# A longer ring of weight chunks in the expert stage of a two-block transformer kernel

## The reference, cut to what matters

```python
g_gate, g_idx = lax.top_k(softmax(t @ w_rg + b_rg), 1)            # best of 4 groups
e_w, e_idx = lax.top_k(softmax(e_logits_of_that_group), 2)        # best 2 of its 8 experts
combine = sum(one_hot(expert_id, 32) * weight[..., None], axis=1)
hid = silu(einsum('td,edf->tef', tk, w1)) * einsum('td,edf->tef', tk, w3)   # 1024 -> 256
hid = hid * c[:, :, None]
y = einsum('tef,efd->td', hid, w2)                                # 256 -> 1024
```

## Time and profile before

| | |
|---|---|
| time, median of 3 runs | 1983.52 us (1982.03 to 1984.95) |
| the profiled execution | 1986.33 us, its span 1984.3 us |
| TensorE matmul busy | 1829.4 us, 92% of the span |
| VectorE / ScalarE / GpSimd busy | 900.6 / 590.2 / 719.3 us |
| HBM read / written | 248.11 / 16.78 MB |
| chain that ended last | TensorE 84%, VectorE 7%, DMA 4% |
| granted TensorE clock, mean | 0.960 |

### The profile page before, as it was taken

One profiled execution on the slowest core, in us unless ns is written; L12 is line 12 of the kernel. 1 busy time (PEld: TensorE's weight loads), 2 busy tenths in 40 slices (PEclk: granted clock), 3 DMA queues, 4 the chain that ended last, 5 costly groups with the idle time before them and its releaser, 6 DMA issues.

```text
span 1984.3 us, 22984 instructions
## 1 busy us (share of the span) xinstructions
PE 1829.4 (92%) x8562; PEld 1338.8 (67%) x8562; DVE 900.6 (45%) x1267; ACT 590.2 (30%) x1085; POOL 719.3 (36%) x413
## 2 busy tenths in 40 slices
PE   5999979999997898898789898999988979999999
PEld 3888757776875343433367776777766868888887
DVE  4220666664534132322333465999647664303331
ACT  2322334453332111010123234555435222212221
POOL 4444323333430000000023236788743425444442
PEclk8999989998997899999979898999998989999999
DMA  5222212223332789898632323121243313222221
GB/s 193 96 84 91 81 64 80 80 83 130 117 122 71 286 312 338 313 338 322 250 128 85 127 85 101 64 80 66 69 167 125 128 53 117 96 96 96 96 96 43
DMA packets 82660, 266.33 MB, mean 134 GB/s; under 512 B 9088, under 2 KB 10112, under 8 KB 82560
## 3 DMA queue, kind: packets, MB, share of 16 engines
q1 hardware_dynamic: 61632, 222.33, 32.6%
q10 hardware_dynamic: 18624, 34.21, 4.9%
q0 software_dynamic: 2304, 8.39, 1.3%
HBM read 248.11 MB, written 16.78 MB: 133 GB/s over the span
## 4 chain that ended last, share of the span: by engine, by line
PE 84%; DVE 7%; DMA 4%; issue 2%; ACT 2%; ACTq 1%; SPq 0%; POOL 0%; DVEq 0%
PE psum L519 81%; DMA ring<-stream 4%; DVE root L1728 1%; PE psum L1106 1%; DVE area_r L1702 1%; ACTq L1639 1%; PE psum L816 1%; PE psum L610 1%; DVE area L2232 1%; DVE root L1707 1%; ACT root L1249 0%; ACT area L1249 0%; DMA area<-xT 0%; DVE yt_lo L2041 0%; PE psum L777 0%
## 5 line engine op out<-in xcount | busy, mean ns | idle before, releaser
L519 PE MATMUL psum<-area_r,ring_hi 128*128 128x512 f32 (+1 forms) x3168 | 1001.5, 398 | 18.2 <-DVE area_r L1702 11.7
L420 POOL TENSOR_TENSOR ring_lo<-ring,ring_hi 128x1024 fp32r<-128x1024 f32 x220 | 534.3, 2432 | 1003.0 <-ACT ring_hi L1249 1003.0
L519 PEld LDWEIGHTS psum<-area_r,ring_hi 128*128 128x128 f32 x3168 | 595.1, 191 | 162.9 <-issue 28.0
L519 PE MATMUL psum<-area_r,ring_lo 128*128 128x512 f32 (+1 forms) x1584 | 621.3, 392 | 0.0
L1249 ACT ACTIVATE ring_hi<-ring 128x1024 fp32r<-128x1024 f32 x220 | 231.8, 1057 | 625.2 <-PE psum L519 596.8
L519 PEld LDWEIGHTS psum<-area_r,ring_lo 128*128 128x128 f32 x1584 | 302.0, 191 | 63.3
L519 PE MATMUL psum<-ring,area 128*64 128x512 f32 x768 | 190.5, 620 | 46.1 <-DMA ring<-stream 19.9
L1249 ACT ACTIVATE area<-psum 128x512 f32<-128x512 f32 (+3 forms) x257 | 124.9, 512 | 202.0 <-PE psum L610 71.4
L1728 DVE RECIPROCAL root<-root 128x512 f32<-128x512 f32 (+1 forms) x30 | 94.1, 3137 | 137.9 <-ACT root L1249 137.9
L519 PEld LDWEIGHTS psum<-ring,area 128*64 128x64 f32 x768 | 51.2, 139 | 143.9 <-issue 136.1
L519 PE MATMUL psum<-area 128*64 128x128 f32 (+6 forms) x832 | 112.1, 346 | 15.9 <-DVE area L1729 9.7
(11 more groups left out here) (209 smaller groups left out, 1579.7 us busy)
## 6 DMA issues: line engine op xcount, KB each, us to landing
ring<-stream SPq DMA_DIRECT2D x420, 512.0 KB, 3.8
area<-gates ACTq DMA_DIRECT2D x40, 256.0 KB, 6.2
gates<-root ACTq DMA_DIRECT2D x24, 256.0 KB, 2.0
gates<-area ACTq DMA_DIRECT2D x16, 256.0 KB, 3.6
area<-xT SPq DMA_DIRECT2D x8, 256.0 KB, 8.1
area<-xT ACTq DMA_DIRECT2D x8, 256.0 KB, 3.3
tokens<-area ACTq DMA_DIRECT2D x2, 1024.0 KB, 4.2
x_kept<-area ACTq DMA_DIRECT2D x8, 256.0 KB, 5.6
```

The source lines that it names most:

```text
L420: nc.gpsimd.tensor_tensor(ring_lo[:, c % RS, :], ring[:, c % R, :], ring_hi[:, c % RS, :].bitcast(F32), ALU.subtract).then_inc(w_lo, 1)
L519: return nc.tensor.matmul(out, lhsT, rhs, start=first, stop=last)
```

## The change

The expert stage gets a ring of twelve chunks (`RM = 12`): the six slots of `ring`, one pair of slots over the unused end of `ring_lo`, and two pairs over the tiles of `xt`. Chunks of the first six places are loaded one by one as before; those of the last six are loaded two at a time, by one DMA of 1 MB into a pair of slots, with a semaphore for each pair (`more0` to `more2`). The first of these is issued when chunk 79 has been used, the other two when the turned tokens have been written to HBM (`tok_kept`). The second buffer of fetched rows goes, since `xt` is now taken; each of the four parts of the one buffer is fetched again when the previous group's rows in it have been transposed. The broadcast weights of `dense` move to other tiles. Many semaphores are shared (`z_out` and `g1_out` become `bank_read`, `x1_out` and `x3_out` become `x_added`, `va_out` and `vb_out` become `v_out`, `lam_ok` is counted in `lam_e`, `g1_in` and `g2_in` become `gates_in`, `x_spilled` is counted in `stored`), with their counts shifted.

```diff
+RM = 12
+def landed(c):
+    if c < MOE0:
+        return c // R + 1
+    if c < MOE1:
+        return (MOE0 + (c - MOE0) % RM) // R + (c - MOE0) // RM + 1
+    return c // R + 1 - (MOE1 - MOE0) // R + (MOE1 - MOE0) // RM
...
-        rows_in = [area[:, b:b + 8, :].rearrange("p (q a) b -> p q (a b)", q=PAIRS) for b in (24, 16)]
+        rows_in = area[:, 24:32, :].rearrange("p (q a) b -> p q (a b)", q=PAIRS)
...
+        ring2 = [nc.alloc_sbuf_tensor_at(f"more{x}", [P, 2, CH], F32, offset=at) for x, at in enumerate(
+            (high_at + 4 * 512 * (NT + 2 * PAIRS), area_at + 2048 * XT, area_at + 2048 * (XT + 4)))]
...
-            segment(MOE0 + R, MOE1 + R, weights_used, R - 1)
+            def load_two(c, x):
+                sp.dma_start(ring2[x][:], stream[bass.ds(c, 2)].rearrange("a p n -> p a n")).then_inc(S(f"more{x}"), 16)
+            sp.wait_ge(weights_used, MOE0)
+            load_two(MOE0 + R, 0)
+            sp.wait_ge(S("tok_kept"), 32)
+            for x in (1, 2):
+                load_two(MOE0 + R + 2 * x, x)
+            with sp.Fori(0, (MOE1 - MOE0) // RM - 1) as t:
+                for i in range(R):
+                    sp.wait_ge(weights_used, t * RM + (MOE0 + i + 1))
+                    load(t * RM + (MOE0 + RM + i), (MOE0 + i) % R)
+                for x in range(3):
+                    sp.wait_ge(weights_used, t * RM + (MOE0 + R + 2 * x + 2))
+                    load_two(t * RM + (MOE0 + RM + R + 2 * x), x)
+            for c in range(MOE1, MOE1 + R):
+                sp.wait_ge(weights_used, c - RM + 1)
+                load(c, c % R)
...
-                    if g >= 2:
-                        pool.wait_ge(S("sp_g"), 2 * PAIRS * (g - 1))
+                    if g:
+                        pool.wait_ge(S("sp_g"), 2 * (PAIRS * (g - 1) + q + 1))
...
-                    pe.wait_ge(loads[c % R], 16 * (c // R + 1))
-                    return ring[:, c % R, :]
+                    return arrived(c, 0)
...
+            def arrived(c, turns):
+                i = (c - MOE0) % RM
+                if i < R:
+                    pe.wait_ge(loads[(MOE0 + i) % R], 16 * landed(c) + turns)
+                    return ring[:, (MOE0 + i) % R, :]
+                x, half = divmod(i - R, 2)
+                pe.wait_ge(S(f"more{x}"), 16 * ((c - MOE0) // RM + 1) + turns)
+                return ring2[x][:, half, :]
```

More of the change, by code:

```diff
@@ L186, in block_program @@
         VA = K
-        HF, HG, CBT = 48, 8, 16
+        HF, HG, CBT = 48, 8, 24
         SQ1, XG, XT, LS = 48, 32, 16, 56
@@ L237, in block_program @@
         NB = {"n1": 0, "nx": 1, "nm": 2, "nf": 3}
-        for name in ("va_sq", "va_ss", "va_root", "va_out", "u_out", "z_mm", "z_out", "vb_out", "lam_e", "lam_ok",
-                     "gate_raw", "gate_kept0", "gate_kept1", "g1_in", "g1_act", "g1_out", "x1_out", "lg_mm", "rt_max", "rt_exp", "rt_out", "ctt", "ct_out",
+        for name in ("va_sq", "va_ss", "va_root", "v_out", "u_out", "z_mm", "bank_read", "lam_e",
+                     "gate_raw", "gate_kept0", "gate_kept1", "g1_act", "x_added", "lg_mm", "rt_max", "rt_exp", "rt_out", "ctt", "ct_out",
                      "ct_dram_ok", "cb_in", "fb_silu", "fb_c", "fb_hid", "fb_y", "fb_add", "merged",
                      "pos_mm", "consts2", "flag_ok", "x1_sq", "xg", "xt_t", "xt_out", "tok_kept", "lg_act", "lg_t", "rt_root",
-                     "sp_idx", "rows_in0", "rows_in1", "rows_in2", "rows_in3", "fb_sum", "fb_root", "fb_h",
+                     "sp_idx", "more0", "more1", "more2", "rows_in0", "rows_in1", "rows_in2", "rows_in3", "fb_sum", "fb_root", "fb_h",
                      "sp_sel", "sp_t", "sp_selT", "sp_c", "sp_cs", "sp_g", "sp_ga", "sp_gd", "sp_silu", "sp_hid",
@@ L653, in _ @@
                 if g >= 4:
-                    pe.wait_ge(S("z_out"), g - 3)
+                    pe.wait_ge(S("bank_read"), g - 3)
                 for c in range(NT):
@@ L662, in _ @@
                 if hf:
-                    pe.wait_ge(S("z_out"), 8)
+                    pe.wait_ge(S("bank_read"), 8)
                 token_major(C0["vb"] + 4 * hf, 4 * hf, tokens(HH1, HL1), NT, lambda k: None)
-            pe.wait_ge(S("vb_out"), 4)
+            pe.wait_ge(S("v_out"), 12)
             normed("qk", qk_entries())
@@ L952, in dense @@
                                     c = C0["moe"] + GC[step, p] + 2 * kp + ex
-                                    pe.wait_ge(loads[c % R], g * (16 * CPG // R) + 16 * (c // R + 1))
+                                    w13 = arrived(c, g * (16 * CPG // RM))
                                     for f in range(FE):
@@ L957, in dense @@
                                                 off = 512 * (k % 2) + 256 * w + P * f
-                                                ins = mm(psum[:, 4 * ex + 2 * f + w, :], ring[:, c % R, off:off + P],
+                                                ins = mm(psum[:, 4 * ex + 2 * f + w, :], w13[:, off:off + P],
                                                          tile(HF + k), k == 0, k == KD - 1)
@@ L968, in dense @@
                                     if m == 0:
-                                        pe.wait_ge(loads[c % R], g * (16 * CPG // R) + 16 * (c // R + 1))
+                                        w2s[x] = arrived(c, g * (16 * CPG // RM))
                                     f, ex = divmod(x, 2)
-                                    ins = mm(psum[:, 4 + m % 4, :], ring[:, c % R, P * m:P * m + P],
+                                    ins = mm(psum[:, 4 + m % 4, :], w2s[x][:, P * m:P * m + P],
                                              tile(HG + 4 * (p % 2) + FE * ex + f), x == 0, x == 3)
@@ L1022, in _ @@
                     c = CMP0 + 4 * kv + q
-                    pe.wait_ge(loads[c % R], 16 * (c // R + 1))
+                    pe.wait_ge(loads[c % R], 16 * landed(c))
                     for l in range(4):
@@ L1253, in high @@
             def high(c):
-                act.wait_ge(loads[c % R], 16 * (c // R + 1))
+                act.wait_ge(loads[c % R], 16 * landed(c))
                 A(ring_hi[:, c % RS, :], ring[:, c % R, :], ACT.Copy).then_inc(w_hi, 1)
@@ L1654, in _ @@
             sigmoids(0)
-            act.wait_ge(S("x_spilled"), 16 * KD)
+            act.wait_ge(S("stored"), 16 * KD)
             for p in range(4):
```

75 lines of the change are left out of this document (38 added, 37 removed).

## The result

| | before | changed |
|---|---|---|
| median of 4 runs each | 1982.78 us (1978.54 to 1984.95) | 1936.27 us (1935.83 to 1938.46) |
| profiled execution / span | 1986.33 / 1984.3 us | 1938.46 / 1936.5 us |

The ratio is 0.9763, 95% interval 0.9742 to 0.9785: faster by 46.5 us between the medians and 47.9 between the profiled executions, where 38 were forecast. Measured once more with other runs of the kernel before (experiment 5), the same kernel took 1940.58 us against 1980.24, ratio 0.9797 (0.9767 to 0.9827): 39.7 us faster.

The account below looks back on a forecast made before the run. In the expert stage neither TensorE nor DMA was full; the two waited for each other. Gains of 36 us from chunk waits and 2 from the clock, off 1986.33, gave 1948.3 us (1945.5 on the median), range 1936 to 1961.

Parts of the forecast that it names:

- chunk waits before, drawn and hidden: Expert stage: TensorE's waits for chunks, 39.2 us drawn plus 0.23 us hidden in each of 34, 47.0 us.
- chunk waits left: Expert stage with twelve slots: 11 us of TensorE's chunk waits stay, so 36 us are gained.
- clock in the stage: Group 0 of the expert stage: half clock behind the 5.6 us wait goes, gain 2 us, between 0 and 3.
- ahead of the stage: Before the expert stage: the three early loads meet the tokens' last write for 1 us at most, cost 0.
- behind the stage: After the expert stage: chunks 272 on may load earlier, but the next stage begins with the norm on VectorE, 0.
- the ledger: Expert stage: TensorE needs 285 us, DMA 268 us for 100.7 MB at 376 GB/s; uneven pace leaves the remaining waits.
- The early loads: Three loads into new slots, issued from 611 us, end by 628, before the first fetch at 630.05: cost 0.
- The one row buffer and the semaphores: Expert stage fetches never wait for the single buffer, 0, above 2 us; merged semaphores change no order, 0 within 0.5.
- Rivals 1 and 4: Expert stage: DMA keeps 319 GB/s, 1977 us; or new slots in effect fill only once, 1975 us; together chance 0.08.
- 2 (new waits on `yt_hi` and `yt_lo`: Expert stage: late work of ScalarE and VectorE is bared, 18 us come back, 1963 us; chance 0.10.
- 3 (the pairs run badly): Expert stage: paired 1 MB loads run at 250 GB/s, stage 16 us longer, 2000 us; chance 0.04.
- the signs of being right: Expert stage 290 to 298 us, chunk waits under 15, DMA 350 to 370 GB/s, remaining waits in group 3's fast stretch.

Follow-up runs that it names:

- experiment 5: The changed kernel, unaltered, run again beside other runs of the kernel before: 1940.58 us, ratio 0.9797.
- Experiment 4: Changed kernel with each of the three new pairs of slots loaded by two DMAs of 512 KB instead of one of 1 MB: 1939.26 us, ratio 0.977.
- experiment 2: Changed kernel with a ring of eight instead of twelve, only the pair over the end of `ring_lo` added: 1952.39 us, ratio 0.984.
- experiment 1: Changed kernel with a ring of six again, the rest of the change kept: 1985.98 us, ratio 1.0011 against the kernel before.

## Why the prediction was off

The direction and the mechanism were right: with more slots most of the chunk waits went, and no other wait took their place. The size, 38 us for 46.5, was not. By the terms of the sum, for the profiled execution of the kernel before against two of the changed kernel, its first and that of experiment 5:

| term | forecast | first profile | second profile |
|---|---|---|---|
| chunk waits before, drawn and hidden | 47.0 | 47.0 | 47.0 |
| chunk waits left | 11 | 5.4 + 9 x 0.23 = 7.5 | 3.8 + 7 x 0.23 = 5.4 |
| clock in the stage, the remainder of its time | 2 | about 6 | about 2.5 |
| ahead of the stage | 0 | -0.1 | 1.7 |
| behind the stage | 0 | 2.2 | 0.1 |
| gain | 38 | 47.9 | 45.9 |

The second stage lasts from 646.8 to 934.9 us. Three terms make up the miss of the first profile, 9.9 us, and the chunk waits left are 3.5 of it. They are the one term that is too large in both profiles.

**Chunk waits left: the step that failed.** The 11 us were 3.5 for group 0, 2 for the middle groups, 2.5 for group 3 and 3 for slots that return in twos and landings that wobble. With the hidden part the two profiles have 3.5 and 1.6 us in group 0, none in the middle groups, and 4.0 and 3.8 in group 3. So the 5 us that stood on no row (middle groups, twos and wobble) were too much; only the 1.3 to 1.5 us that group 3 has over its share can belong to them.

The rate behind the ledger was too low. It took 1.39 us a chunk, from 376 GB/s in what I called full stretches. With twelve slots DMA moves 409 to 417 GB/s in the stage, 1.28 us a chunk, and its volume is 246 us instead of 268, which leaves TensorE 39 us of slack on the average and not 17. The five microseconds at the kernel's start had shown that rate (410), and I set it aside. The stage before had it too, for a few microseconds at a time, as at the end of the longest wait:

```profile
666.20:669.60 3.40, 1.38 (x4) 0.59 (x6) 0.00 (x0) 0.00 (x0) 0.00 (x0) 0.52 1.02 411
```

So six slots don't forbid the rate; they don't keep it up. The best 10 us of the stage before move about 400 GB/s and the best 20 about 375, those with eight and twelve slots 412 to 417 over either. A busy share of 1.00 to 1.02 stood beside 365 to 384 GB/s and beside 411 alike. That the queue runs short inside such stretches, with some 3 chunks in flight of six, is my reading; no view counts what an engine has queued. The means over the stage (319, 350 and 363 GB/s with six, eight and twelve slots) say nothing on this, for the bytes are the same and the mean only tells the stage's time again. Experiment 4 shows that the rate doesn't come from the larger transfers.

For group 3 two errors of the ledger worked against each other. At 1.28 us a chunk its fast stretch lacks 26 x (1.28 - 0.91) = 9.6 us. A lead of 12 x 1.28 less the 5.6 us in flight before is 9.8 and would leave nothing; less the 7.4 us in flight now it is 8.0, and 1.6 us are missing, where 2.8 drawn stand. The same picture, a lead near nothing with six slots to which each slot adds its transfer time, makes the first slots worth most, as experiment 2 found; but it had said 1955 to 1962 us for eight slots, and 1952.39 were measured, so it is a rough one.

**The clock: under-sized, and in part luck.** Only the half clock behind the longest wait was counted. In the kernel before 20.5 us of the stage are at half clock (by the granted clocks of the earlier trace rows, 0.91, 0.98, 0.98 and 1.00, about as much), in the changed kernel's first profile 3.4. One stretch of 6.8 us stands behind the longest chunk wait, also in experiment 1, and is gone with twelve slots; the one at 652.7 doesn't go with the ring, since experiment 5 has it. There the first profile has 43 records where that of before has 27; at 0.215 us a record (1.71 us for eight) that is 3.4 us. In the eight profiled executions with twelve slots and the selection matmuls in one piece the stage has 3.4 to 20.5 us at half clock, 13.7 in the middle: the first profile is the luckiest of them. The 3.4 us, and the 4.3 between the two medians of one kernel, can't be given to the change. With the second ratio, 0.9797, the forecast's 0.981 lies inside the interval; the change is worth 40 to 47 us.

**Behind the stage.** From the end of the stage to the end of the kernel the first profile is 2.2 us shorter than that of before. It has less half clock there: its two long stretches right behind the stage are 10.2 us each, and 13.7 before. I priced it at 0 and know of no cause in the change; experiment 5 has 13.7 again with the ring of twelve, and its kernel behind the stage is only 0.1 us shorter. So this is a matter of the run too.

**What was right.** The early loads cost nothing that can be seen: DMA moves 225 GB/s in 611 to 616, 243 in 616 to 620 and 211 in 620 to 630, the first fetch is issued at 629.86 as before (630.05), and the stage begins at 648.5 in both (lines of the changed kernel, columns as in the earlier trace rows):

```profile
611.00:616.00 5.00, 3.52 (x20) 1.31 (x18) 1.64 (x5) 2.98 (x6) 0.00 (x0) 1.00 0.64 225
616.00:620.00 4.00, 0.00 (x0) 0.00 (x0) 3.49 (x17) 1.18 (x3) 0.00 (x0) 0.79 0.65 243
620.00:630.00 10.00, 6.96 (x33) 6.96 (x33) 7.62 (x29) 1.69 (x3) 0.14 (x1) 0.50 0.57 211
```

The one row buffer and the semaphores cost nothing that can be measured (experiment 1). Rivals 1 and 4 (DMA's pace stays, head start only), 2 (new waits on `yt_hi` and `yt_lo`: still 3.1 us in 2) and 3 (the pairs run badly) didn't come. Of the signs of being right, DMA's 350 to 370 GB/s came (363), and the stage was shorter than the 290 to 298 us given (286.5 and 288.1). The remaining waits stand only in part where these signs had them: 2.6 us of the 5.4 follow the first fetch (655 to 690), and 2.8 lie in group 3. The Trainium skill's figure for a single 1 MB transfer ("DMA: Bandwidth & Descriptors", "Bandwidth": 341 GB/s) would have led further astray; its 425 GB/s for 16 MB is near the 409 to 417 of twelve slots here.

## What to carry to other kernels

Take the rate of a transfer queue from a stretch in which many loads are waiting in it, as at this kernel's start, and not from stretches picked by their busy share: near 1.0 the share went with 365 GB/s and with 411 here. As a rough picture, one more slot in a ring adds its transfer time to a lead that is the ring less the time in flight; where that lead is near zero, the first slots bring most (two of the six new ones brought 32 of 40 to 47 us). Of a sum's terms, those that stand on no row deserve the widest bounds. Other transfers on the same engines, here a fetch of 2.1 MB, must be counted against the lead. Where runs of one kernel differ by several microseconds, compare the stretches at half clock before a difference of that size is given to a change.

## What the runs showed of the hardware

- In stretches of 10 us with a DMA share of 1.00 to 1.02 the core moved 365 to 384 GB/s with a ring of six; over 3.4 us it moved 411 at a share of 1.02 with the same ring, and with twelve slots 409 to 417 at a share of 1.03.
- The time of a load from issue to landing grew with what was queued: for 512 KB 5.6 us with a ring of six and 7.4 with twelve, where it hardly matters, and 3.7 for 256 KB with six.
- TensorE's granted clock fell to one half (1.2 GHz) for 6.8 us while the same small matmuls ran (32 records of 10 columns), from a start between 650.3 and 652.8 us, in nine of the twelve profiled executions in which these stood in one piece, and in three not; with the same program it happened in one execution and not in another.
